# An mLSTM, Fourier and attention stack in fp32: the rows of bounds reach all partitions by DMA through DRAM, and the heads stand two half slots later

## The reference, cut to what matters

```
logw = bcum[..., :, None] - bcum[..., None, :] + lic[..., None, :]
m_new = jnp.maximum(log_prev, jnp.max(logw, axis=-1))
w_intra = jnp.exp(logw - m_new[..., None])
scores = jnp.einsum('bhjd,bhsd->bhjs', qc, kc) * w_intra
den = jnp.sum(scores, axis=-1) + w_prev * jnp.einsum('bhk,bhjk->bhj', nv, qc)
out = num / jnp.maximum(jnp.abs(den), jnp.exp(-m_new))[..., None]
```

## Time and profile before

| what | us |
|---|---|
| runs | 1309.97, 1309.4, 1305.73; median 1309.4 |
| profiled execution | 1305.76 |
| its span | 1303.9 |
| TensorE busy (matmuls) | 1231.4, 94% of the span |
| VectorE busy | 872.8, 67% |
| ScalarE busy | 600.5, 46% |
| GpSimd busy | 209.3, 16% |
| mean granted TensorE clock | 0.983 of full |

### The profile page before, as it was taken

The page is one execution under the profiler, slowest core; times in us unless marked ns, Lnnn a source line. Parts: engine busy times, 40 slices in busy tenths (PEclk is TensorE's granted clock), DMA queues, the critical chain, the costliest instruction groups (busy, mean ns, idle before and its releaser), DMA issues.

```text
span 1303.9 us, 22450 instructions
## 1 busy us (share of the span) xinstructions
PE 1231.4 (94%) x9124; PEld 1128.7 (87%) x9124; DVE 872.8 (67%) x1346; ACT 600.5 (46%) x900; POOL 209.3 (16%) x147
## 2 busy tenths in 40 slices
PE   4799999999999999998999999999989789999996
PEld 1577777777888899998999989999978778999996
DVE  2778844436878877764448878665468996876644
ACT  3423343336656445553244354454364555444433
POOL 1334400000000000001100322220004961222100
PEclk9799999999999999999999999999999889999999
DMA  9566311112322236552154445555524303554550
GB/s 390 229 251 239 149 66 65 66 65 97 130 98 98 97 130 211 194 189 97 35 192 165 162 149 190 178 191 192 180 97 148 130 33 132 189 193 168 189 194 33
DMA packets 27474, 195.57 MB, mean 150 GB/s; under 512 B 3192, under 2 KB 3328, under 8 KB 3968
## 3 DMA queue, kind: packets, MB, share of 16 engines
q1 hardware_dynamic: 26496, 191.90, 41.0%
q10 hardware_dynamic: 896, 2.50, 0.5%
HBM read 193.33 MB, written 1.05 MB: 149 GB/s over the span
## 4 chain that ended last, share of the span: by engine, by line
PE 82%; DVE 10%; ACT 4%; issue 1%; POOL 0%; ACTq 0%; DVEq 0%
PE ps L421 24%; PE ps L422 24%; PE ps L423 24%; DVE acc L2107 3%; PE ps L446 3%; PE ps L642 2%; DVE w_lo L1497 2%; PE ps L542 1%; PE ps L630 1%; PE ps L461 1%; DVE xconv L1603 1%; ACT x_hi L1210 1%; ACT w_hi L925 1%; PE ps L692 1%; DVE xconv L1576 0%
## 5 line engine op out<-in xcount | busy, mean ns | idle before, releaser
L1497 DVE TENSOR_TENSOR w_lo<-ring,w_hi 128x1024 fp32r<-128x1024 f32 x288 | 356.3, 1256 | 173.9 <-ACT w_hi L925 166.7
L925 ACT ACTIVATE w_hi<-ring 128x1024 fp32r<-128x1024 f32 x312 | 323.6, 1054 | 313.2 <-PE ps L423 233.2
L421 PE MATMUL ps<-x_hi,w_hi 128*128 128x258 f32 (+1 forms) x1216 | 346.4, 285 | 7.6 <-DVE x_lo L1838 4.1
L422 PE MATMUL ps<-x_lo,w_hi 128*128 128x258 f32 (+1 forms) x1216 | 344.0, 283 | 0.0
L423 PE MATMUL ps<-x_hi,w_lo 128*128 128x258 f32 (+1 forms) x1216 | 343.7, 283 | 0.0
L421 PEld LDWEIGHTS ps<-x_hi,w_hi 128*128 128x128 f32 x1216 | 230.9, 190 | 11.0 <-issue 10.8
L422 PEld LDWEIGHTS ps<-x_lo,w_hi 128*128 128x128 f32 x1216 | 231.2, 190 | 0.1
L423 PEld LDWEIGHTS ps<-x_hi,w_lo 128*128 128x128 f32 x1216 | 230.8, 190 | 0.0
L421 PE MATMUL ps<-g_hi,w_hi 128*128 128x256 f32 x608 | 171.0, 281 | 3.1 <-POOL g_lo L1441 1.7
L423 PE MATMUL ps<-g_hi,w_lo 128*128 128x256 f32 x608 | 170.3, 280 | 0.0
L422 PE MATMUL ps<-g_lo,w_hi 128*128 128x256 f32 x608 | 170.3, 280 | 0.0
(11 more groups left out here) (310 smaller groups left out, 1964.9 us busy)
## 6 DMA issues: line engine op xcount, KB each, us to landing
ring<-in_weights SPq DMA_DIRECT2D x156, 1024.0 KB, 4.8
o_sb<-in_weights SPq DMA_DIRECT2D x10, 1024.0 KB, 6.4
ada_room<-in_weights SPq DMA_DIRECT2D x10, 1024.0 KB, 6.8
V<-in_weights SPq DMA_DIRECT2D x3, 1024.0 KB, 22.5
dft<-in_dft ACTq DMA_DIRECT2D x1, 1026.0 KB, 7.2
X<-in_x SPq DMA_DIRECT2D x1, 1024.0 KB, 5.0
ctx_room<-in_ctx SPq DMA_DIRECT2D x1, 1024.0 KB, 7.5
xconv<-in_weights SPq DMA_DIRECT2D x1, 1024.0 KB, 27.4
```

Of the source, the lines that this page charges most:

```text
L421: mm(dst, w_h, x_h, start=start, stop=False, skip_group_check=True)
L422: mm(dst, w_h, x_l, start=False, stop=False, skip_group_check=True)
L925: do(w_hi[:, q % 2, part], ring[:, q % RING, part], ACT.Copy).then_inc(S("hi_ready"), 1)
L1497: v.tensor_tensor(w_lo[:, q % 2, part], ring[:, q % RING, part], w_hi[:, q % 2, part], ALU.subtract).then_inc(S("lo_ready"), 1)
```

## The change

Three things. First, `spread` is no longer a pair of matmuls: ScalarE writes the rows of all heads (16 KB) to an internal DRAM tensor once, waits for that, and then for each head issues two DMAs that read the head's rows with a step of 0 over 128 partitions, one into the new tile `floor_of` (bounds), one into `em` (floors), 256 KB each. ScalarE's exponentials and VectorE's masked sums read `floor_of` in place of PSUM, and ScalarE's copy of the floors (line 1105) is gone, as is GpSimd's clearing of `room`. The selection matrix, with two small matrices behind it that this stage does not read either, is no longer loaded (448 of 978 columns of `cst` remain). Second, on TensorE every head starts two half slots later: `at` is `13 + 6n`, and 11 in place of 13 halves follow the last head. Third, on VectorE `mask_diagonals(0)` stands behind `lo(5)` and `apply_z(0)` in place of ahead of them. The other orders of VectorE and ScalarE are as they were.

```diff
-        cst = sb("cst", (P, CSTS))
+        cst = sb("cst", (P, CST["select"][0]))
+        floor_of = sa("floor_of", (P, 2, SEQ))
+        floors = nc.dram_tensor("floors", (HEADS, 4, SEQ), F32, kind="Internal").ap()
@@ TensorE
-            def spread(hd):
-                if hd:
-                    pe.wait_ge(S("diag_ready"), hd)
-                    pe.wait_ge(S("wexp_ready"), hd)
-                else:
-                    pe.wait_ge(S("floor_ready"), 1)
-                sel = cc("select", hd * P, (hd + 1) * P)
-                mm(ps[:, 0, :], sel, room[:, 4:6, :], start=True, stop=True)
-                mm(ps[:, 1, :], sel, room[:, 6:8, :], start=True, stop=True).then_inc(S("spread_done"), 1)
             halves(0, 7)
             columns()
-            halves(7, 8)
-            spread(0)
-            halves(8, 11)
+            halves(7, 13)
             for n in range(HEADS):
-                at = 11 + 6 * n
+                at = 13 + 6 * n
                 denominators(n)
                 halves(at, at + 3)
-                if n + 1 < HEADS:
-                    spread(n + 1)
                 mix_values(n)
...
-            halves(11 + 6 * HEADS, 2 * (N_OZ + N_MOUT))
+            halves(13 + 6 * HEADS, 2 * (N_OZ + N_MOUT))
@@ ScalarE
-            act.dma_start(cst[:, :], cst_in).then_inc(S("ident_ready"), 16)
+            act.dma_start(cst[:, :], cst_in[:, 0:CST["select"][0]]).then_inc(S("ident_ready"), 16)
             def weigh(hd):
-                act.wait_ge(S("spread_done"), hd + 1)
+                act.wait_ge(S("spread_loaded"), 32 * (hd + 1))
...
-                chain.step(do(em[hd % 2], ps[:, 1, :].rearrange("p (d j) -> p d j", d=2), ACT.Copy))
                 act.wait_ge(S("diag_ready"), hd + 1)
-                    chain.step(do(w[:, d, t, lo:hi], ps[:, 0, d * SEQ + lo:d * SEQ + hi], ACT.Exp,
+                    chain.step(do(w[:, d, t, lo:hi], floor_of[:, d, lo:hi], ACT.Exp,
                                   bias=gcol[:, d, t, hd:hd + 1]))
...
                 last.then_inc(S("wexp_ready"), 1)
+                if hd + 1 < HEADS:
+                    act.wait_ge(S("wexp_ready"), hd + 1)
+                    act.wait_ge(S("diag_ready"), hd + 1)
+                    spread(hd + 1)
+            def spread(hd):
+                if hd >= 2:
+                    act.wait_ge(S("probs_ready"), hd - 1)
+                for dst, at in ((floor_of[:, :, :], 0), (em[hd % 2], 2)):
+                    act.dma_start(dst, floors[hd:hd + 1, at:at + 2, :].broadcast_to([P, 2, SEQ]))\
+                        .then_inc(S("spread_loaded"), 16)
             do(grow(3)[:, 0], grow(3)[:, 0], ACT.Exp, scale=-1.0).then_inc(S("floor_ready"), 1)
+            act.wait_ge(S("floor_ready"), 1)
+            act.dma_start(floors, room[0:HEADS, 4:8, :]).then_inc(S("floors_kept"), 16)
             next_slot(3)
+            act.wait_ge(S("floors_kept"), 16)
+            spread(0)
             weigh(0)
@@ GpSimd
-            nc.gpsimd.memset(room[:, 4:8, :], 0.0).then_inc(S("spread_clear"), 1)
@@ VectorE
-            dve.wait_ge(S("spread_clear"), 1)
             def mask_diagonals(hd):
-                dve.wait_ge(S("spread_done"), hd + 1)
+                dve.wait_ge(S("spread_loaded"), 32 * (hd + 1))
...
-                    ins = v.scalar_tensor_tensor(wexp[hd % 2][:, d, t, lo:lo + P], ps[:, 0, d * SEQ + lo:d * SEQ + lo + P],
+                    ins = v.scalar_tensor_tensor(wexp[hd % 2][:, d, t, lo:lo + P], floor_of[:, d, lo:lo + P],
-            mask_diagonals(0)
             lo(STARTS["oz"] + 5)
             apply_z(0)
+            mask_diagonals(0)
             apply_z(1)
             weigh_scores(0)
```

## The result

The changed kernel took 1381.0 us in the median of 6 runs (1377.38 to 1382.38), the kernel before 1310.05 (1305.73 to 1311.31): a ratio of 1.054, interval 1.0519 to 1.0561. The forecast was 1363, the range ended at 1377. The direction and the cause were as forecast; the size was not, and the time lies above the range.

The account below looks back on a forecast made before the run. The prediction took TensorE, busy 94% of the span, as the bound. Its terms, -6.9 + 27.6 + 6.8 + 14.8 + 3.4 + 6.0 + 4.2 = +55.9 on 1305.8, gave 1361.7, plus 1.3 for the median: 1363, range 1346 to 1377.

Parts of the forecast that it names:

- First stalls: In each of four heads TensorE waits 6.9 us ahead of half 14+6n for a lo queued behind normalise: +27.6 us.
- Second stalls: Ahead of half 18+6n TensorE waits 3.4 us in heads 0 and 1, 4.0 in heads 2 and 3: +14.8 us.
- Tail: Behind the last head, half 40 waits 4.3 us for lo(20), plus 1.7 for a half-clock return: +6.0 us.
- Clock behind the long stalls: TensorE's clock returning after each of the four 6.9 us waits costs 1.7 us: +6.8; 1.7 more behind the last head.
- Clock after the shorter stalls: Clock loss behind the wait at the start and the four of 3.4 to 4.0 us: +4.2, bounds 0 and 8.5.
- Start of head 0: Half 12 waits 3.8 us on the chain from head 0's broadcast, less 0.4 waited before: +3.4, bounds +2.7 and +8.
- Constants and layout: At the kernel's start, the constants' load shrinks by 0.27 MB: at most 1.3 us less, taken as 0.
- A: Rival: the change works, TensorE remains the bound, the sum is -6.9 us, 1302.5; chance 0.03.
- B: Rival: drops cancel, only one or two heads stall and the time stays within 0.3%; chance 0.01.
- C: Rival: in the heads only the stall at half 14 occurs and the clock hardly falls: +28, 1334 to 1338; chance 0.06.
- E: Rival: a broadcast or store over 8 us shifts only the start by 5 or more, 1368 to 1380; chance 0.04.
- D: Rival: the clock stays low between the heads' gaps, another 4 us lost in each head, +16, 1378; chance 0.06.

Follow-up runs that it names:

- e2: The changed kernel with TensorE's heads back at their old place, two halves earlier; 1311.91 us, ratio 1.0022.
- e10: The kernel before, its orders unchanged, with the matmul spread kept for head 0 and the DMA through DRAM for heads 1 to 3; 1305.88 us, ratio 0.9964.
- e7: The changed kernel with one line of VectorE's order moved, lo(7+3n) ahead of normalise(n); 1341.08 us, ratio 1.0234.
- e6: The changed kernel with unused matmuls on TensorE filling most of each wait; 1355.53 us, ratio 1.0346.
- e1: The kernel before with TensorE's heads two halves later and the matmul spread kept; 1379.06 us, ratio 1.053.
- e11: The changed kernel with the broadcast's target in an existing tile and 530 unused columns, so every tile lies where it lay before; 1379.4 us, ratio 1.0526.
- e3: The changed kernel with the orders of VectorE and ScalarE moved by one slot as well; 1310.34 us, ratio 0.9999.
- e5: The kernel before with an unused tile of 14 columns behind the constants; 1311.08 us, ratio 1.0002.
- e9: The changed kernel with VectorE's and ScalarE's orders moved too, 18 unused columns, head 0's broadcast issued earlier and move_oz(15) moved earlier; 1309.28 us, ratio 1.0004.

## Why the prediction went wrong

The steps, in their order:

- *Eight spread groups, -6.9*: held. The heads came 1.7 us closer (e2), 31.1 in place of 32.8, and 1.5 in e10.
- *First stalls, +27.6*: 27.9 (6.96, 6.93, 6.95, 7.08). Held, with its mechanism; e7 takes them away by one line.
- *Second stalls, +14.8*: 14.8 (3.40, 3.40, 4.10, 3.93). Held, with the releasers named for each head.
- *Tail, a stall of 4.3*: 4.13. Held.
- *Clock behind the long stalls, +6.8 and 1.7 in the tail*: 8.7 and 2.5, short by 2.7. The 1.7 taken for each is an estimate that no run shows; the nearest row is one sum that took 3.50 us in place of 1.73. The runs showed 1.8 to 2.5 behind the four (two halves in 7.77 to 8.46 us, in e6 in 5.9 to 6.0) and 2.5 in the tail. A return could last over 4 us: 0.53 over six of them, above.
- ***Clock after the shorter stalls, +4.2: failed, 11.1*** (8.7 behind the second stalls, 2.4 at the start). I bounded it by 0 and 8.5 and took the middle. The upper bound, five times that 1.7, was no bound: a wait of 3.4 cost as much as one of 7, or more (2.4 each in three of four, against 1.8 to 2.5). All ten returns were charged, 1.5 to 2.6 us each, with the granted clock at 0.50 behind every one. The free wait of 2.25 us that spoke for the low end was the wrong neighbour. The one of 2.37 us ahead of 316.02, in the changed kernel, was free too (48 matmuls in 5.94 us, 1.00), but the wait there, 2.25 to 2.45 long, left the clock at 0.72 over the next six microseconds in seven of the twelve kernels (e1 to e6 and e11).
- ***Start of head 0, +3.4: failed, 8.5*** (8.94 less 0.4). TensorE was ready when forecast (340.2, forecast 335.3 plus the 5.1 by which the stage began later). The broadcast landed 6.3 us after its issue, not 3.3, and its issue began earlier than I had it by 0.9: +2.1. ScalarE's table load (339.85, 1.28 long) came only behind its wait for the masks, whereas I had counted it as done ahead: +1.3. The move of `o_sb` out of PSUM, which half 12 also needs, stood behind `hi(6)` and a table load of 1.28: +1.1. With 0.2 for the exponentials that is 4.7 of the 5.1.
- ***Constants and layout, 0 to -1.3: failed, +5.1 ahead of the heads.*** From the first of the twelve groups to the o/z stage it is 239.7 us against 235.7, +4.0 (nine groups at 0.34 and three at 0.7 are 5.2, and the wait for `qk_lo` is 0.95 shorter); the first 1.1 lie in the start-up, where the first of these groups began anywhere from 59.6 to 62.7 in the twelve kernels. I priced the removed bytes and not the moved addresses.
- *Later broadcasts hidden, the stretch behind 500 as before*: held. No wait of heads 1 to 3 ends on the broadcast, and behind the stage it is -0.9.
- *The distance from one head's denominators to the next, 43 us*: 46.6, 45.8 and 46.6, longer by the clock terms.

Adding up: +5.1 ahead, +5.1 start, +6.9 and +2.7 clock, +0.3 first stalls, -0.2 tail, -0.9 behind, and 1.7 of the heads that I can put nowhere make the 20.7 us between 55.9 and 76.6. So no rival took the forecast's place: the terms were too small. Of the rivals, A and B fell with the ten waits. C fell with the second waits, which stood in the changed kernel. E needed a broadcast of over 8 us, and the slowest took 6.3 in the changed kernel and 7.6 in e2, e3 and e10. D came close in its time, 1378, but at another 4 us lost in each head, where each return cost 1.5 to 2.6.

The range failed because bounds were too narrow, not because they were combined wrongly. Its end, 1377, is already the forecast with every term at its upper bound (1361.7, 11.8 and the median's 3.6), although the prediction says that they don't all fall one way. Outside their bounds lay the clock behind the shorter stalls (11.1, bound 8.5), that behind the long ones (8.7, bound 8), the start (8.5, bound 8) and what stands ahead of the heads (5.1, bound 0). The two clock bounds were one unknown, the price of a return.

DMA issues behind the start, 325 to 345 in the changed kernel (KB, median us to landing). Of the two pairs in it, that of head 0 took 5.8 and 6.3 while a 1 MB load was under way, that of head 1 took 3.0 and 3.4; over all four heads the medians are 3.5 and 4.1.

```profile
ring<-in_weights SPq DMA_DIRECT2D x2, 1024.0 KB, 5.7
floor_of<-floors ACTq DMA_DIRECT2D x2, 256.0 KB, 4.4
V<-floors ACTq DMA_DIRECT2D x2, 256.0 KB, 4.8
```

## What to carry to other kernels

When a producer that others wait for is moved on one engine, move the orders of all engines that feed it, or check for each operand which wait it now stands behind (with all orders moved, e3 took 1310.34 us in place of 1381.0). Count the returns of the clock, not the length of the waits, and treat their price as one unknown for all: here it was 1.5 to 2.6 us behind waits of 3.4 to 8.9. A DMA in place of a matmul paid here where something else hid its whole trip, the store to DRAM included: in the later heads (e10, 4.5 us less), and not in the first (e2, where TensorE waited 9.58 us ahead of it).

## What the chip showed that I had not expected

- In these kernels the pace of the 512-column matmuls depends on where the tiles lie in SBUF: 232.8 ns each (11.17 us for 48) in the layout of before, 235 (11.28) with e5's 14 columns and 239.8 (11.51) in the changed kernel's. Which tile and which distance decide it stays open; e5 refuted my guess. In the whole time the difference does not show clearly.
- In the changed kernel waits of 3.4 us and of 7 us cost about the same at the return, 1.5 to 2.6 us. Waits of 1.83 to 1.93 us for `qk_lo` cost 1.6 us in four profiled executions, and waits of 1.80 in two others cost nothing. Those of 2.25 to 2.45 ahead of half 4 left the granted clock at 1.00 over the next six microseconds in five kernels (before, the changed one, e7, e9, e10) and at 0.72 in the seven others, where in e6 that cost 1.5 us.
- A broadcast of 256 KB from DRAM to all partitions landed 3.5 (bounds) or 4.1 us (floors) after its issue (medians of the changed kernel), up to 6.3 there while a 1 MB load was under way, and 7.6 in e2, e3 and e10. The 16 KB store ahead of it took 4.2 (e9).
- Exponentials of 128 by 256 read from SBUF were slower than from PSUM: six took 2.29 to 2.30 us in each of the four heads of the changed kernel, before 2.08.
